# A two-network kernel: norms of four plain networks, the end of the recurrent mixer, and the norm between the last two streams rearranged

## What is computed

```python
def rms_norm(x, g, eps=NORM_EPS):
    x32 = x.astype(jnp.float32)
    y = x32 * lax.rsqrt(jnp.mean(x32 * x32, axis=-1, keepdims=True) + eps)
    return (y * g.astype(jnp.float32)).astype(x.dtype)

def swiglu(h, w_gate, w_up, w_down):
    return (jax.nn.silu(h @ w_gate) * (h @ w_up)) @ w_down

# first block, each layer: x + 0.5*swiglu(norm(x)); a mixer; x + 0.5*swiglu(norm(x))
# layer 0 mixes with attention, layer 1 with the recurrent mixer, which ends so:
def rwkv7_time_mix(h, ...):
    g = jax.nn.sigmoid(xg @ g1) @ g2            # g1: 1024 x 160, g2: 160 x 1024
    ...
    _, y = lax.scan(rwkv7_step, state, seqs)
    mu = jnp.mean(y, axis=-1, keepdims=True)    # over the 64 columns of a head
    var = jnp.mean(jnp.square(y - mu), axis=-1, keepdims=True)
    y = ((y - mu) * lax.rsqrt(var + GN_EPS)).reshape(B, S, D)
    y = y * lnx_g.astype(f32) + lnx_b.astype(f32)
    y = y + (jnp.sum(r_h * k_h * r_k.astype(f32), axis=-1, keepdims=True) * v_h).reshape(B, S, D)
    return (y.astype(h.dtype) * g) @ w_o

# second block, each layer, for the tokens x and the context xc:
h = modulate(rms_norm_2(x, g_norm1[layer]), sh1, sc1)
hc = modulate(rms_norm_2(xc, g_norm1[layer]), csh1, csc1)
glu, gate, (qm, km, vm), (qg, kg, vg) = project_tokens(h, p, rope_m, rope_g)
glu_c, gate_c, (qmc, kmc, vmc), (qgc, kgc, vgc) = project_tokens(hc, p, None, None)
# attention over context and tokens, merge, x + ...; then x + g2 * conv_ffn(...)
# in the last layer the context gives its keys and values only
```

## Time and profile before

| | us |
|---|---|
| median of 3 runs | 2786.09 |
| lowest, highest | 2786.03, 2791.97 |
| the profiled execution's own time | 2789.98 |
| its span, first to last instruction | 2788.2 |
| TensorE busy in it | 2725.2 |
| VectorE busy | 2104.0 |
| ScalarE busy | 1290.8 |
| TensorE's mean granted clock | 0.996 of full |

### The profile page before, as it was taken

The page is one execution under the profiler, slowest core; times in us unless marked ns, Lnnn a source line. Parts: engine busy times, 40 slices in busy tenths (PEclk is TensorE's granted clock), DMA queues, the critical chain, the costliest instruction groups (busy, mean ns, idle before and its releaser), DMA issues.

```text
span 2788.2 us, 51351 instructions
## 1 busy us (share of the span) xinstructions
PE 2725.2 (98%) x20666; PEld 2514.9 (90%) x20666; DVE 2104.0 (75%) x3185; ACT 1290.8 (46%) x1777; POOL 110.2 (4%) x109
## 2 busy tenths in 40 slices
PE   8999999999999999999999999999999999999999
PEld 8998799999888979999969999985999989859998
DVE  6885589889755637994977877698787856987777
ACT  5345543443532215344555445456454454564443
POOL 0000000000014300000000000000000000000000
PEclk9999999999999999999999999999999999999999
DMA  7754267667431025764414554440344524403454
GB/s 264 271 226 158 89 254 275 246 231 273 148 122 60 1 78 219 272 227 166 164 57 158 179 183 178 154 150 18 137 166 181 179 108 151 151 16 137 166 181 151
DMA packets 61231, 456.23 MB, mean 164 GB/s; under 512 B 6840, under 2 KB 6864, under 8 KB 8736
## 3 DMA queue, kind: packets, MB, share of 16 engines
q1 hardware_dynamic: 54432, 395.83, 39.4%
q0 software_dynamic: 6656, 58.35, 5.2%
HBM read 453.09 MB, written 1.07 MB: 163 GB/s over the span
## 4 chain that ended last, share of the span: by engine, by line
PE 83%; DVE 11%; ACT 3%; DMA 2%; issue 1%; DVEq 0%; SPq 0%; ACTq 0%
PE ps L744 19%; PE ps L592 14%; PE ps L593 14%; PE ps L594 14%; PE ps L1021 3%; PE ps L1393 2%; DMA ring<-in_weights 2%; PE ps L542 2%; DVE half_parts L2254 1%; DVE arena L2659 1%; PE ps L1256 1%; PE ps L1110 1%; PE ps L1103 1%; DVE w_parts L2061 1%; ACT arena L1990 1%
## 5 line engine op out<-in xcount | busy, mean ns | idle before, releaser
L1544 ACT ACTIVATE w_parts<-ring 128x1024 fp32r<-128x1024 f32 x462 | 462.9, 1051 | 427.1 <-PE ps L592 300.4
L2061 DVE SCALAR_TENSOR_TENSOR w_parts<-ring,w_parts 128x1024 fp32r<-128x1024 f32 x462 | 544.2, 1219 | 76.5 <-ACT w_parts L1544 76.5
L744 PE MATMUL ps<-stream_high,half_parts 128*128 128x256 f32 x2224 | 425.4, 287 | 1.7 <-DVE half_parts L2254 1.7
L2254 DVE SCALAR_TENSOR_TENSOR half_parts<-ring,half_parts 128x1024 fp32r<-128x1024 f32 x225 | 271.6, 1212 | 169.3 <-ACT half_parts L1631 168.8
L744 PEld LDWEIGHTS ps<-stream_high,half_parts 128*128 128x128 f32 x2224 | 350.7, 189 | 6.9 <-issue 6.1
L592 PE MATMUL ps<-act_parts,w_parts 128*128 128x256 f32 x1232 | 346.9, 282 | 7.2 <-DVE act_parts L2061 4.0
L594 PE MATMUL ps<-act_parts,w_parts 128*128 128x256 f32 x1232 | 348.0, 282 | 0.0
L593 PE MATMUL ps<-act_parts,w_parts 128*128 128x256 f32 x1232 | 347.8, 282 | 0.0
L592 PE MATMUL ps<-h_parts,w_parts 128*128 128x256 f32 x1200 | 341.1, 284 | 1.5 <-DVE w_parts L2061 1.5
L593 PE MATMUL ps<-h_parts,w_parts 128*128 128x256 f32 x1200 | 339.5, 283 | 0.0
L594 PE MATMUL ps<-h_parts,w_parts 128*128 128x256 f32 x1200 | 339.5, 283 | 0.0
(11 more groups left out here) (442 smaller groups left out, 5230.3 us busy)
## 6 DMA issues: line engine op xcount, KB each, us to landing
ring<-in_weights SPq DMA_DIRECT2D x374, 1024.0 KB, 4.8
arena<-in_mod_weights POOLq DMA_DIRECT2D x32, 1536.0 KB, 8.3
arena<-in_cond POOLq DMA_DIRECT2D x8, 512.0 KB, 6.6
arena<-toeplitz_rows POOLq DMA_DIRECT2D x1, 1536.0 KB, 10.8
x<-in_x SPq DMA_DIRECT2D x1, 1024.0 KB, 4.9
arena<-in_ctx POOLq DMA_DIRECT2D x1, 1024.0 KB, 5.1
out<-x SPq DMA_DIRECT2D x1, 1024.0 KB, 3.9
const<-in_const SPq DMA_DIRECT2D x1, 975.0 KB, 11.3
```

What stands on the lines that cost most here:

```text
L744: mm = pe.matmul(into, stationary, moving, start=start and n == 0, stop=stop and n == 2, skip_group_check=True)
L1544: a(w_parts[:, to, 0, cols], ring[:, at, cols], ACT.Copy).then_inc(s["w_high"], 1)
L2061: return stt(out=out, in0=whole, scalar=1.0, in1=high, op0=ALU.mult, op1=ALU.subtract)
L2254: stt(out=half_parts[:, u % 3, 1, :], in0=ring[:, (t["tile"] + tile) % RING, half * HALF:(half + 1) * HALF], scalar=1.0, in1=half_parts[:, ...
```

## The change

Line numbers of the diff are those of the two files; the functions are the same.

In the **plain networks**, VectorE adds the eight slices of squares to two before TensorE sums them (`add_squares`, `added_norm`: two products with ones in place of eight), and that sum stands behind the up product of tile 1. The banks are not cleared; the first product into each of them begins a sum. VectorE makes the remainder of tile 2 ahead of the reciprocal.

In the **attention**, three products of constants stand ahead of the last weighing.

In the **recurrent mixer**, the gate's inner width is done as two blocks of 128 (the weights beyond 160 are zeros already), chunk 0's outputs are copied by ScalarE, the sums of squares stand inside the second pair of g, the spread is made from two rounded halves of the inverses with its last pair put off into the output projection, and four products of constants are added.

In the **streams**, stream 3's norm, its high and low halves and its first weight halves are made inside stream 2; stream 2's head sums (L1348) follow stream 3's opening; all the products of constants there go.

```diff
             def added_norm(count, bank, squares):
+                pe.wait_ge(s["squares_added"], count)
+                for k in range(2):
+                    mm = pe.matmul(ps[:, bank, 0:S], C("ones"), squares[:, k, :], start=(k == 0), stop=(k == 1))
+                mm.then_inc(s["ss_ready"], 1)
...
+                        opens = plain and isinstance(j, int) and j == r == m % 2 == 0
                         first, mm = product(t, r * KT + m, ps[:, 4 + m // 2, (m % 2) * S:(m % 2 + 1) * S],
-                                            act_parts[:, buf, 0, cols], act_parts[:, buf, 1, cols], False, last and r == 1)
+                                            act_parts[:, buf, 0, cols], act_parts[:, buf, 1, cols], opens, last and r == 1)
...
                 if plain:
                     plain_gate().then_inc(s["gate_ready"], 1)
+                    project(1, 0, 1, h_parts).then_inc(s["up_ready"], 1)
                     if n == 0:
                         pe.wait_ge(s["const_loaded"], 16)
-                    norm(h_need - 1, 2)
-                    project(1, 0, 1, h_parts).then_inc(s["up_ready"], 1)
+                    else:
+                        pe.wait_ge(s["x_ready"], (0, 2, 3, 5)[n] * QUARTERS)
+                    added_norm(n + 1, 3, norm_sq)
                     if ahead is not None:
-                        norm(ahead, 3, h)
-                    if n:
-                        pe.wait_ge(s["x_ready"], (0, 2, 3, 5)[n] * QUARTERS)
-                    clear_sums()
-                    pe.wait_ge(s["std_ready"], h_need)
+                        added_norm(n + 2, 4, h)
                     pair(0, 0, h_parts)
...
+                pe.wait_ge(s["dl_pt"], 3)
+                warm(4, 3)
                 weigh((2, 3))
...
-                narrow(5, (128, 32))
+                narrow(5, (P, P))
...
+                widen_pair(g_lora, (P, P))
+                widen_pair(g_lora, (P, P), among=square_sums)
+                for p in range(2):
+                    widen_pair(g_lora, (P, P))
+                pe.wait_ge(s["mm_evac"], mm_n[0] - 3)
+                warm(mm_n[0] % 4, 1)
+                spread_pairs((0, 1, 2))
                 pe.wait_ge(s["mm_evac"], mm_n[0])
+                warm(mm_n[0] % 4, 3)
                 for q in range(3):
                     pe.wait_ge(s["y_ready"], q + 1)
+                    if q == 1:
+                        spread_pairs((3,))
...
-                split_opening(i + 1, filler=(i == 3))
+                split_opening(i + 1, filler=False)
+                if i == 3:
+                    latent_key_sums(STREAMS[2])
...
-                    warm(5, 7)
+                    norm(NORMS[3], 5)
...
             for t in STREAMS:
-                if t["i"] == 3:
-                    warm(3, 8)
-                    pe.wait_ge(*left[3])
-                    norm(NORMS[3])
                 stream(t)
...
+                    if m == 2:
+                        for g in range(2):
+                            actv.wait_ge(s["rw_y"], g + 1)
+                            a(y[:, 4 * g:4 * g + 4, 0:P], ps[:, g, :].rearrange("p (m t) -> p m t", m=4), ACT.Copy).then_inc(s["rw_ys"], 1)
...
+                if not full:
+                    squares(STREAMS[3]["x"], needs(STREAMS[3]), norm_sq)
...
+                if not full:
+                    high_halves(STREAMS[3], 1)
+                    norm_root(NORMS[3], 5, 1)
+                    high_halves(STREAMS[3], 2)
...
+                def add_squares(v, count):
+                    dve.wait_ge(s["sq_ready"], QUARTERS * count)
+                    for at in (0, 4):
+                        link.mark(tt(v[:, at:at + 2, :], v[:, at:at + 2, :], v[:, at + 2:at + 4, :], ALU.add))
+                    link.wait()
+                    tt(v[:, 0:2, :], v[:, 0:2, :], v[:, 4:6, :], ALU.add).then_inc(s["squares_added"], 1)
...
                 low(1)
+                add_squares(norm_sq, h_need)
+                if ahead:
+                    add_squares(h, NORMS[ahead["i"]] + 1)
+                low(2)
                 dve.wait_ge(s["std_ready"], h_need)
                 link(nc.vector.reciprocal(rstd[:, 0, 0:S], std[:, 0, 0:S]))
                 scale_gate(0)
-                low(2)
                 scaled_activation(0)
                 low(3)
...
+                if not full:
+                    open_ahead(STREAMS[i + 1])
```

147 lines of the change are left out of this document (89 added, 58 removed).

## The result

| | before | changed |
|---|---|---|
| median of the runs shown | 2789.03 (4 runs) | 2760.06 (4 runs) |
| lowest, highest | 2786.03, 2793.19 | 2756.59, 2764.08 |
| profiled execution, own time | 2789.98 | 2756.59 |
| its span | 2788.2 | 2754.8 |
| TensorE busy | 2725.2 | 2692.3 |

The account below looks back on a forecast made before the run. TensorE was taken as the bound: its work, clock and where it stands. Savings of 10.7 + 1.7 + 0 + 8.5 + 19.1 = 40.0 us turned span 2788.2 into 2748.2, execution 2750.0, median 2746; range 2737 to 2757.

Parts of the forecast that it names:

- Plain networks: The four plain networks' openings: earlier tile 4 starts save 10.7 us, bounds 6 and 17.6, despite a new 1.7 us stall.
- G: In each plain network, the end of the first gate, from which the forecast counts tile starts: tile 3 at + 14.1.
- The transfer: In the plain networks, tile 3's weight transfer, beside 4 MB of modulation weights, landing no earlier: low bound of 6 us.
- Attention: Last weighing: three constants fill the 1.31 us idle; 1.7 us go if the clock holds, 0 if it falls.
- Copies of chunk 0: Recurrent mixer: ScalarE's copies delay the masks as VectorE's had, one wait replacing another; 0 us, other bound 3.4.
- Mixer: Recurrent mixer's whole blocks, narrow change, spread and sums of squares: 2.9 + 0.4 + 5.1 + 0.1 = 8.5 us saved, bounds 5 and 9.
- the narrow product: Recurrent mixer: `narrow` changes once instead of alternating with whole blocks, a saving of 0.4 us.
- the row: Profile row for the mixer's g pairs: mixed 128 and 32 rows take 2.31 to 2.51 us, whole ones should take 1.73.
- Between the streams: From stream 2's keys to stream 3's first whole product: 2264.9 in place of 2284.01, 19.1 us saved, bounds 16 and 20.
- The sum: Whole kernel: 10.7 + 1.7 + 0 + 8.5 + 19.1 = 40.0 us saved, span 2748.2 from 2788.2.
- Rival 3: Stalls of 1.7 us make the clock fall, four costing 2 each: 2754, or 2757; chance 0.24 together with failing covers.
- The step from execution to median: Whole kernel: the profiled execution lies 3.9 us above the median of 2786.1, so 2750.0 becomes a median of 2746.

## Why the prediction was wrong, point by point

**Plain networks: right.** Tile 3 at G + 14.1 in all three that had no second sum, with the wait of 1.8 us foreseen as 1.7; tile 4 in network 0 at 39.51 = 19.31 + 20.2, as forecast. Network 0 gave 1.5 of 1.7 by its tile 4, network 3 gave 5.0 of 5.0. In networks 1 and 2 the falls behind tile 3 took most of it back: by their tile 4 they had given 1.0 of 2.3 and 0.2 of 1.7. The transfer, named as the reason for the low bound, was nearer to deciding than the text said: it alone would have held tile 3 until 554.03 + 1.05 + 1.2 and a hand-over of 0.1, G + 13.4.

**Attention: right.** The weighing takes 2.19 us in place of 3.85. Of five traces here that lack the three constants, three have a fall at the weighing; of the thirteen that have them, none. So the 1.7 us are worth about 1 us on average (an estimate, 1.7 x 3/5).

**Copies of chunk 0: right in its mechanism.** The wait ahead of chunk 1's last group is 1.77 where it was 1.74, the masks following L1816 as forecast. The group behind it takes 2.33 in place of 2.76, because this time the clock held; it also holds in the trace of the mixer's part alone, where VectorE still copies. Nothing of it is the change's, and the low clock that made the 2.76 stands in one of the 18 traces only.

**Mixer: 6.6 in place of 8.1 (without the narrow product).** Pairs and sums take 10.96 from 1001.22 to 1012.18, where they took 13.39: 2.4, not 3.0; spread, constants and projection 25.2 where they took 29.4: 4.2, not 5.1. Several terms are a little too small: in the first part the whole pairs, 7.3 where 6.9 stood, and the sums, 3.66 where 3.45 stood; in the second the products of 16 rows (twelve and four took 1.62 + 0.67 = 2.3 where 1.9 stood), the constants (1.92 where 1.7 stood) and the projection (0.3 more). The clock stayed at full in the spread and the projection, as forecast. Sixteen whole products of g take 7.3 us where the mixed ones took 9.8, so filling up the 32 rows gave 2.5 us. The Trainium skill's rule that a dimension of 32 or less can run up to four times faster ("TensorEngine Tiling (Array Packing)", section "Theoretical Speedup") did not come to bear, as the row had said. The Trainium skill also says, in "TensorE: Matmul & The Clock Gate", section "Why this matters for your kernels", that a single product with a contraction of 32 takes the time of one of 128; the 0.47 at 16 rows beside 0.43 at 128 is the nearest that was measured here and roughly agrees; the 0.63 in alternation is dearer than either.

**Between the streams: right** to 0.1 us, and the first ten halves of stream 3 have no wait of 0.4 or more.

**The sum: wrong, in what it took the clock to be.** The forecast read three falls in one trace (at 330, 1020 and 2272 us), put their recovery (by the measure above 1.7 + 5.1 + 1.7 = 8.5 us) into its terms as gains, and took all else to stay at full clock. That leaves 10.3 - 8.5 = 1.8 us of loss. The trace after has 10.3, so the step is off by 8.5. The first half of it was right: none of the three falls is in any trace of the new code. The second half failed: two falls stand behind the new idles at tile 3 (3.4 us of loss), and four at places that the change didn't touch (6.8 us), where the trace of before has none; its one other fall, 1.7 us at 941, is gone. Everything else is, taken together, better than forecast by 1.9, and two late weight tiles of network 0 that didn't come are 1.7 of that: 40.0 - 8.5 + 1.9 = 33.4. (These splits go by the loss as counted, which is more than the cost at some places.)

The falls at untouched places are drawn anew in every execution: three traces of the same program lose 10.3, 18.8 and 10.2, and other traces of kernels with the old code have some of them too (264 and 295 us in that of the networks' part alone). A fall that is seen once at a place is worth its price times its chance, which was 4 of 4 at the old spread and 2 of 4 ahead of stream 3, and the places at which nothing was seen have a chance too. Rival 3 was the right mechanism for one half of it: filling the new idles gives back 5 us in the median (2759.2 against 2753.9). It was given 2 us for each of four networks, but stood beside the forecast as a case apart, instead of in the sum with its chance, of which the traces show 8 in 16. The other half, the falls at untouched places, no rival had.

**The step from execution to median** was made with three runs. Their median, 2786.09, is at the low end of what the kernel before does: the larger series here have medians of 2789.85 (16 runs), 2788.88 (15), 2790.51 (11) and 2787.70 (11). To take off 3.9 us for it was to lean on a number with an uncertainty of 3; the range had no room for that. On the other side the profiled execution of the changed kernel happened to be 3.5 under its median.

**Which version is best.** With four constants ahead of tile 3, 2754.5 and 2753.9 in two series, ratios of 0.9869 and 0.9885: 34 to 36 us under the kernel before and some 5 under the changed one.

## What to carry to other kernels

Read two or three traces of the same program before a fall of the clock is put into a sum: one execution shows which falls happened, not which belong to the place, and a change that removes an idle in one place and makes a shorter one in another can come out even. Where a step is moved ahead to shorten a wait, follow it back to the transfer that feeds it, on every engine that touches it: tile 3 was held by VectorE's chain and, 0.7 us behind, by a transfer, and each order that cured the first ran into the second. A wait that can't be removed can be filled, and here products of constants that put tile 4 back by 0.3 us in one network of four gave 5 in the median. A sum of low clock over a trace is a bound on what the clock cost: to know the cost, compare the starts of the same instruction ahead of the fall and behind it in two traces.

## What the runs showed of the hardware

Three traces of the same program have a loss by the clock of 10.2 to 18.8 us, by falls at places that differ. A fall that counts 6.8 us where TensorE also waits for VectorE cost 4.0 in position; one that counts 1.7 in dense products behind tile 3 cost 1.3 at tile 4. The spans less this loss lie within 0.4 us of each other (2744.5, 2744.6, 2744.9), which is partly luck, since in the second 3.2 us of other delays, late weight tiles among them, were offset by such overcounting. The idles at tile 3, 0.9 to 2.2 us, are followed by low clock in 8 of 16 cases (all four in network 1, three of four in network 2, none of the four in network 0, none of the three under 1.1 us in network 3), and the same time filled with products in none of 24. The clock falls without any idle where products of 16 rows follow one another: by chance behind 2.85 and 3.72 us of them, and at all three places of the one trace that has twice that. Behind the old spread of the mixer (eight full products, 16 rows deep) it fell in four of four traces, and behind the new one, of twelve rounded products, in none of 14. Products of 128 rows and of 16 in alternation have a pace of 0.63 us each, against 0.43 and 0.47 among their like.
